# Feed-forward stages with one 512-column matmul for both activation parts, and a mixer whose silu gates stand before the attention

## The reference, cut to what matters

```python
def swiglu(h, w_gate, w_up, w_down):                 # four times, and once more in layer 0 of the second block
    return (jax.nn.silu(h @ w_gate) * (h @ w_up)) @ w_down      # 1024 -> 2816 -> 1024

# even mixer (once): three attention branches, softmax(q @ k.T * scale + mask) @ v, and a gated unit
# mixer of the second block (twice), from proj = h @ w_in[layer]:
y_a = (silu(rg) * rms_norm(retention(rq, rk, rv))) @ ret_w_out
y_b = (silu(hg) * rms_norm(hgrn2_scan(...)) * norm_g) @ hgrn_w_out
y_c = swa_with_sinks(sq, sk, sv, sinks) @ swa_w_out              # softmax attention, 16 heads
merged = sigmoid(ga) * y_a + sigmoid(gb) * y_b + sigmoid(gc) * y_c
mix = merged @ w_o
```

## Time and profile before

| what | value |
|---|---|
| median of three runs | 3395.35 us |
| the profiled execution | 3393.7 us |
| its span | 3391.8 us |
| mean granted TensorE clock | 0.961 |
| VectorE busy | 2269.6 us |
| ScalarE busy | 1820.6 us |

### The profile page before, as it was taken

The page is one execution under the profiler, slowest core; times in us unless marked ns, Lnnn a source line. Parts: engine busy times, 40 slices in busy tenths (PEclk is TensorE's granted clock), DMA queues, the critical chain, the costliest instruction groups (busy, mean ns, idle before and its releaser), DMA issues. The chain is left out here.

```text
span 3391.8 us, 49440 instructions
## 1 busy us (share of the span) xinstructions
PE 3141.8 (93%) x20206; PEld 2824.7 (83%) x20206; DVE 2269.6 (67%) x2478; ACT 1820.6 (54%) x2143; POOL 175.6 (5%) x101
## 2 busy tenths in 40 slices
PE   6998799998999899989899999897999999999996
PEld 6987699887689799879898998896888888888885
DVE  3455445787744556565545556645899899999997
ACT  3444444433244455464344455552777777777775
POOL 0000000002400001010000020100000000000000
PEclk9998899999999899989999999997999999999998
DMA  4552155443145433334454433333999999999995
GB/s 154 185 190 108 72 178 201 174 173 124 63 174 185 180 131 132 131 109 152 171 186 161 141 134 126 126 137 149 339 355 361 353 353 358 351 356 349 355 364 196
DMA packets 97410, 698.58 MB, mean 206 GB/s; under 512 B 10960, under 2 KB 11472, under 8 KB 13776
## 3 DMA queue, kind: packets, MB, share of 16 engines
q1 hardware_dynamic: 97232, 696.11, 56.5%
HBM read 693.97 MB, written 1.05 MB: 205 GB/s over the span
## 5 line engine op out<-in xcount | busy, mean ns | idle before, releaser
L854 PE MATMUL ps<-act_high,weight_low 128*128 128x256 f32 x3072 | 878.3, 286 | 0.0
L854 PE MATMUL ps<-act_high,weight_high 128*128 128x256 f32 x2624 | 757.0, 288 | 24.3 <-DVE weight_low L710 16.7
L854 PE MATMUL ps<-act_low,weight_high 128*128 128x256 f32 x2624 | 749.4, 286 | 0.0
L854 PEld LDWEIGHTS ps<-act_high,weight_low 128*128 128x128 f32 x3072 | 599.0, 195 | 0.0
L854 PEld LDWEIGHTS ps<-act_high,weight_high 128*128 128x128 f32 x2624 | 511.1, 195 | 34.9 <-issue 18.5
L854 PE MATMUL ps<-weight_low,act_high 128*128 128x512 f32 (+2 forms) x1456 | 515.3, 354 | 0.0
L854 PEld LDWEIGHTS ps<-act_low,weight_high 128*128 128x128 f32 x2624 | 511.1, 195 | 2.3 <-issue 0.2
L854 PE MATMUL ps<-weight_high,act_high 128*128 128x512 f32 (+2 forms) x1360 | 496.3, 365 | 13.7 <-DVE act_low L2655 3.9
L854 PE MATMUL ps<-weight_high,act_low 128*128 128x512 f32 (+2 forms) x1360 | 487.6, 359 | 0.0
L710 DVE TENSOR_TENSOR weight_low<-ring,weight_high 128x2048 fp32r<-128x2048 f32 x108 | 247.4, 2291 | 245.6 <-ACT weight_high L663 245.5
L663 ACT ACTIVATE weight_high<-ring 128x2048 fp32r<-128x2048 f32 x108 | 206.6, 1914 | 351.5 <-PE ps L854 351.5
(11 more groups left out here) (447 smaller groups left out, 5764.3 us busy)
## 6 DMA issues: line engine op xcount, KB each, us to landing
ring<-in_l_moe_up SPq DMA_DIRECT2D x110, 1024.0 KB, 6.0
ring_more<-in_l_moe_down SPq DMA_DIRECT2D x110, 1024.0 KB, 6.0
ring<-in_l_w_in SPq DMA_DIRECT2D x92, 1024.0 KB, 4.8
vtm<-in_l_moe_gate SPq DMA_DIRECT2D x55, 1024.0 KB, 6.0
merged<-in_l_moe_gate SPq DMA_DIRECT2D x55, 1024.0 KB, 6.1
ring<-in_l_ffn_down SPq DMA_DIRECT2D x52, 1024.0 KB, 4.8
ring<-in_l_ffn_up SPq DMA_DIRECT2D x35, 1024.0 KB, 4.8
ring_more<-in_l_ffn_gate SPq DMA_DIRECT2D x32, 1024.0 KB, 4.8
```

The costliest lines, as they stand in the source:

```text
L854: ins = nc.tensor.matmul(out, still[a], moving[b], start=first and n == 0, stop=last and n == 2, skip_group_check=True)
```

## The change

1. **Feed-forward, gate and up.** `act_high` and `act_low` become one tensor `c.act` (k, part, 256). One matmul `both_parts` moves 512 columns, high and low side by side, under the high weight into a whole bank; `high_part` moves 256 under the low weight into its first half. So 16 matmuls per half instead of 24. The bank's two halves are then summed by VectorE's `tensor_reduce` over pairs: `gate_sums` for the gate and the same in `products` for the up. ScalarE's silu and VectorE's product read the sums, and TensorE's banks come free with the sums.
2. **Feed-forward, order.** `clear` is gone: the first `down` starts its banks itself (the loop's first two bodies are peeled for that). At the start of a stage the third unit's high and low are made before the silus and the products, not behind them.
3. **Attention.** The next pass's scores wait for `read`, signalled by the mask addition, not for `biased`.
4. **Mixer.** HGATE moves from 38 to 32, SQ, SK, SV to 36, 40, 41, ATTEND from 38 to 42; the four `hg_split` stand at u = 34, 35, 39, 40. The silu gates get buffers of their own. GpSimd's loop is four gates, then eight weighings.
5. **Sigmoid gates** become tanh(x/2): `unload` takes tanh with scale 0.5, VectorE adds 1 in the same instruction that multiplies, and the factor of a half is applied where the merged sum is split.

```diff
@@ split_ffn_stage
-                nc.scalar.activation(silu[h], ps[:, 2 * h, 0:T], ACT.Silu).then_inc(silu_made.sem, 1)
+                nc.scalar.activation(silu[h], gate[h], ACT.Silu).then_inc(silu_made.sem, 1)
...
+            def gate_sums(n):
+                for h in range(2):
+                    dve.wait_ge(made.sem, n * 6 + (mb + h + 1))
+                    dve.wait_ge(silu_made.sem, n * 2 + (sb + h - 1))
+                    nc.vector.tensor_reduce(gate[h], halves(2 * h), axis=AX.X, op=ALU.add)\
+                        .then_inc(gate_made.sem, 1)
             def products(n):
                 for h in range(2):
+                    dve.wait_ge(made.sem, n * 6 + (mb + h + 3))
+                    nc.vector.tensor_reduce(rise[h], halves(2 * h + 1), axis=AX.X, op=ALU.add)\
+                        .then_inc(rise_made.sem, 1)
+                for h in range(2):
                     dve.wait_ge(silu_made.sem, n * 2 + (sb + h + 1))
-                    nc.vector.tensor_tensor(hidden[h], silu[h], ps[:, 2 * h + 1, 0:T], ALU.mult).then_inc(hidden_made.sem, 1)
+                    nc.vector.tensor_tensor(hidden[h], silu[h], rise[h], ALU.mult).then_inc(hidden_made.sem, 1)
...
             def start():
                 make_low(first[1])
+                gate_sums(0)
+                make_low(second)
                 products(0)
-                make_low(second)
             def triple(t):
                 hidden_lows(t.n, t.odd)
                 make_low(t.unit(1))
+                gate_sums(t.n + 1)
                 make_low(t.unit(2))
                 products(t.n + 1)
                 make_low(t.unit(3))
...
+                        both_parts(c, 2 * h + bank, still[0][0], 0)
+                        for k in range(KD):
+                            high_part(c, 2 * h + bank, still[k][1], k)
+                        for k in range(1, KD):
+                            last = both_parts(c, 2 * h + bank, still[k][0], k)
...
+def both_parts(c, bank, still, k):
+    return c.nc.tensor.matmul(c.ps[:, bank, :], still, c.act[:, k, :, :].rearrange("p s t -> p (s t)"), start=k == 0,
+                              stop=k == KD - 1, skip_group_check=True)
+def high_part(c, bank, still, k):
+    return c.nc.tensor.matmul(c.ps[:, bank, 0:T], still, c.act_high[:, k, :], start=False, stop=False, skip_group_check=True)
@@ even_stage and mixer_stage
-                    pe.wait_ge(biased.sem, biased.base + n)
+                    pe.wait_ge(read.sem, read.base + n)
@@ mixer_stage
-RQ, RK, RV, HF, HQ, HI, RG, GA, SQ, SK, SV, HGATE, GB, GC, SO, WO, UNITS = (
-    0, 2, 4, 8, 12, 16, 20, 24, 32, 36, 37, 38, 42, 50, 54, 58, 62)
-ROPE, RETAIN, PREPARE, RECUR, ROOT, ATTEND = 4, 7, (12, 24), (17, 29), (24, 36), 38
+RQ, RK, RV, HF, HQ, HI, RG, GA, HGATE, SQ, SK, SV, GB, GC, SO, WO, UNITS = (
+    0, 2, 4, 8, 12, 16, 20, 24, 32, 36, 40, 41, 42, 50, 54, 58, 62)
+ROPE, RETAIN, PREPARE, RECUR, ROOT, ATTEND = 4, 7, (12, 24), (17, 29), (24, 36), 42
+HG_SPLIT = (34, 35, 39, 40)
...
-                    take(gate[i % 2], ACT.Sigmoid)
+                    half_tanh(gate[i % 2])
```

More of the change, by code:

```diff
@@ L597, in split_ffn_stage @@
     ahead = Ahead(c, then, used) if then is not None else None
-    acts = (c.act_high, c.act_low)
     silu = [c.work[:, T * h:T * h + T] for h in range(2)]
     hidden = [c.work[:, T * (2 + h):T * (3 + h)] for h in range(2)]
+    gate = [c.work[:, T * (4 + h):T * (5 + h)] for h in range(2)]
+    rise = [c.work[:, T * (6 + h):T * (7 + h)] for h in range(2)]
+    halves = lambda bank: ps[:, bank, :].rearrange("p (s t) -> p t s", s=2)
     class Step:
@@ L606, in __init__ @@
             self.n, self.pair, self.odd = pair * 2 + odd, pair, odd
+            self.first = isinstance(pair, int) and pair == 0 and odd == 0
         def unit(self, j):
@@ L618, in stream @@
         else:
-            with eng.Fori(0, G // 2) as i:
+            body(Step(0, 0))
+            body(Step(0, 1))
+            with eng.Fori(1, G // 2) as i:
                 for odd in range(2):
@@ L768, in _ @@
         def _(pe):
[L769 to L773, removed]
             def split(u):
@@ L786, in across, with down @@
                     pe.wait_ge(freed.sem, n * 2 + (count + h - 1))
[L787 to L788 removed]
+                    still = [[m[:, k, P * h:P * h + P] for m in w] for k in range(KD)]
+                    if fresh and h == 0:
+                        for k in range(KD):
                             pe.wait_ge(norm.low.sem, norm.low.base + k + 1)
[L790 to L791 removed]
+                            if k < KD - 1:
+                                both_parts(c, 2 * h + bank, still[k][0], k)
+                            last = high_part(c, 2 * h + bank, still[k][1], k)
+                        last = both_parts(c, 2 * h + bank, still[KD - 1][0], KD - 1)
+                    else:
+                        both_parts(c, 2 * h + bank, still[0][0], 0)
+                        for k in range(KD):
+                            high_part(c, 2 * h + bank, still[k][1], k)
+                        for k in range(1, KD):
+                            last = both_parts(c, 2 * h + bank, still[k][0], k)
                     last.then_inc(made.sem, 3 if h == 1 and last_first else 1)
[L794 removed]
+            def down(u, n, odd, final=False, fresh=False):
                 w = [m.rearrange("p (h n) -> p h n", h=2) for m in split(u)]
@@ L816, in triple @@
                 across(t.unit(1), t.n + 1, 1)
-                down(t.unit(2), t.n, t.odd)
+                down(t.unit(2), t.n, t.odd, fresh=t.first)
             stream(pe, start, triple, lambda: down(after.unit(0), G - 1, 0, True))
@@ L1378, in even_stage @@
         s.advance(2)
-    for s in (scored, biased, exped, factored, weighted, probs, probs_taken, attended):
+    for s in (scored, read, biased, exped, factored, weighted, probs, probs_taken, attended):
         s.advance(PASSED)
```

110 lines of the change are left out of this document (57 added, 53 removed).

## The result

The kernel after takes 3354.62 us (median of four runs, 3353.27 to 3356.12), the kernel before in the same session 3396.9. The ratio is 0.9878, 95% interval 0.9863 to 0.9894. The forecast was 3360 in 3346 to 3391, faster.

A forecast was written before the change was run, and what follows sets the result against it. TensorE, busy 93% of the span, was taken as the bound, VectorE in parts of the third feed-forward stage, ScalarE and VectorE in mixer attention. 3393.7 - 23.5 (feed-forward) - 11 (mixers) = 3359, median said 3360, range 3346 to 3391.

The forecast's parts named there:

- Start: Start of each feed-forward stage: 2.8 us of waiting goes, a new stall of 0.7 comes, net 2.1 per stage.
- Sums: VectorE in feed-forward: 0.69 us per sum, free in four plain stages, third stage 3.5 us longer.
- (a): First body of the third feed-forward stage: a 5.1 us table piece and gate sums delay a low, stall 3.2 us.
- (b): Second body of the third feed-forward stage, with a table piece of 4.1 us: stall 1.1 us.
- Step (c): Third feed-forward stage, two bodies bound by VectorE take its work in full: 2 x 2.7 = 5.3 less TensorE's 0.4.
- (d): Third feed-forward stage, the two bodies behind the VectorE-bound ones, pieces of 2.5 to 3.3 us: about 1 us.
- Mixers: Two mixers' attention: seven steps 74.9 us instead of 78.2, first step about 2.2 shorter; 5.5 per mixer, 11 together.
- bound of 20: Upper bound of the mixers' gain, if TensorE's waits, 7.5 us in one mixer, go too.
- A: Rival: feed-forward sums cost VectorE 1.22 us each, feed-forward gives 3.0, kernel 3381 us; chance 0.10.
- B: Rival: 512-column matmuls cost 0.240 us, fixed price not saved, 22.9 us comes back, kernel 3383; chance 0.06.
- D: Rival: a sum costs 1.75 us, third feed-forward stage grows some 43, kernel 3418; decides from about 1.45; chance 0.05.
- C: Rival: the mixers give nothing, through odd steps' unloads and exps or a late recurrence; kernel 3371 us; chance 0.09.

The follow-up runs named there:

- e6: The kernel after with each 512-column matmul of gate and up made as two of 256 columns: 3376.13 us, ratio 0.994 to before.
- e4: The kernel before with only the start order of the five feed-forward stages changed and the zero matmuls gone: 3379.19 us, ratio 0.9955.
- the second profile: The kernel after once more, unchanged, on the chip of the kernels with even pieces: 3354.58 us, ratio 0.9884 to before.
- e5: The kernel after with each sum over pairs made twice, 1.37 us instead of 0.69: 3373.32 us, ratio 0.9932 to before.
- e9: The kernel after, third feed-forward stage with three 256-column matmuls per k-step, no sums, table instructions in 19 near-even pieces: 3345.11 us.
- e7: The kernel after with the two mixers' gates as ScalarE's Sigmoid again instead of tanh: 3355.05 us, ratio 0.9879 to before.
- e8: The kernel after with the attention's scores waiting for the scaled maximum (`biased`) again: 3355.21 us, ratio 0.988 to before.
- e2: The kernel before with only the attention and mixer part of the change, feed-forward as before: 3383.72 us, ratio 0.9971.
- e11: The kernel before once more, unchanged, for a second profile: 3396.11 us, one run.
- e10: The kernel after, 512-column matmuls and sums kept, third feed-forward stage's table instructions cut into 19 near-even pieces: 3346.56 us, ratio 0.9861 to before.
- e3: The kernel after, third feed-forward stage alone with three 256-column matmuls per k-step and no sums: 3352.61 us, ratio 0.9879 to before.

## Why the prediction was right, point by point

The direction and most terms held. The forecast median was 35 us under that of before; measured are 42 in the same session and 39 to 42 against all runs of before. Feed-forward and mixers gave 33.8 us in the traces where 34.5 were said, but several terms of that sum were off by 1 to 4 us and cancelled, which is luck.

**1. Matmuls.** Forecast 0.227 and a body of 16.55; measured 0.230 between `both_parts` and 16.61 for the bodies of the plain stages, so 0.37 us per body and not 0.43. At 11 groups that is 4.1 per stage and 20.4 in all instead of 22.9. The fixed price is there (e6: bodies of 16.98 again), but it is worth 0.012 us per matmul saved and not 0.013. The 2.5 ns that the Trainium skill ("TensorE: Matmul & The Clock Gate", "Back-to-back issue gap") gives for a matmul by itself would have given a body of 16.9; the trace decides against it.

**2. Start.** No zeros, and the new wait of 0.7 at the second up unit has a start distance of 0.84 us in all five stages, 0.6 above the normal one: as forecast. Net 2.1 was right: 4.1 + 2.1 = 6.2 stands against 6.3 in FF 2, 6.5 in FF 5 and 6.6 in the second profile's FF 1 (201.76; the first profile's 7.5 has 0.9 us more in the same code). In FF 4 the wait of before also cost clock (e4), and windows there would have shown it beforehand; with its 1.7 the stage's 8.0 comes out.

**3. Sums.** 0.685 us each, free in the plain stages (e5), as forecast. In FF 3 the waits (a) and (b) were forecast at 3.2 and 1.1; the start distances are 3.08 and 1.14, so 2.9 and 0.9 as waits. Step (c) was mis-sized: "its work in full: 2 x 2.7" was to add 4.9 us in two bodies. (By its own premise the 0.4 us that TensorE saves in each such body turn into waiting and had to be added, not taken off: 6.2.) TensorE's distances there were 2.67, 1.28 and 1.95 and are 4.33 and 3.33, 1.8 more; above the normal distance that is 2.0. VectorE was not full there: it was idle for 1.35 and 1.13 us of the windows in the earlier trace rows, and e9 shows that with the work cut evenly TensorE does not wait at all. (d) gave nothing (2.07 and 2.10). So waits add 5.8 us and not 10.2. In their place came what the prediction had not: behind the long waits TensorE runs at its lower clock, 4.0 us above before by the 22 and 3 doubled distances. -4.1 - 2.1 + 5.8 + 4.0 = +3.6, measured +4.6; 1 us stays open. That the forecast was +3.5 is luck: two errors that cancel, waits put 4.4 us too high and a clock that was put at nothing. The clock of FF 3 was never taken out by itself; that the waits cause its fall is argued from where it falls, and e6's wait of 3.60 us without a fall shows that it need not.

**4. Mixers.** Seven steps of 74.9 us were forecast, 74.91 is measured, and the single steps are those of the sum: five of 9.33 and 12.1, the first two 10.91 and 9.06, 1.5 us less for the copies that they lack. The step before them is 1.95 shorter, 2.2 was said. 5.2 per mixer by the steps, 5.2 by the length of mixer 1. The bound of 20, that TensorE's waits for the statistics go, was none: they went, but TensorE waited for the turned probabilities beside them already, and does so longer in after. The waits of before there, among them, are 15.9 us together, those of after 13.8. First the two lines of before that the earlier trace rows lacks, then after:

```profile
PE ps L2226 <- ACT rowbuf L2429: 7.2, 3, 2.5
PE ps L2226 <- ACT work L2429: 1.2, 1, 1.2
```

```profile
PE ps L2265 <- ACT rowbuf L2469: 9.1, 3, 3.9
PE ps L2265 <- ACT work L2469: 3.2, 2, 3.0
PE ps L2255 <- DVE work L2677: 1.5, 1, 1.5
```

Tanh gives nothing (e7), the wait for `read` neither (e8), so the order of the units is what is left of the part that e2 tests; no run changes the order alone.

**5. Read wait.** Zero (e8: +0.6, inside the scatter of the runs, 3352.82 to 3357.35).

**What the sum lacked.** 33.8 of the 40.4 us by which the two profiled spans differ are feed-forward and mixers (-23.7 and -10.1 with 4.85 in mixer 2, whose length in before's own two traces is 494.1 and 492.6). 2.3 in the odd stage are its clock, which differs between two executions of the same kernel by more than that (e11). The even mixer's 1.2 and the 3.0 of the experts lie in code that is the same or has no effect, and both are within what these stages differ by from trace to trace: the even mixer has 167.7 to 169.9 us in its new form and 168.8 to 170.3 in its old one, and the experts, whose code is the same in all fourteen traces, 1052 to 1059. Here all of these fell to the change's side; why they differ is open.

The rivals: A, B and D are excluded by the rows (0.685 us per sum, 0.230 per matmul), C by e2. D's threshold was too low (e5), and its 13.3 us of VectorE work in a body of the third stage stand in no row; the earlier trace rows have 15.6 and 15.9.

## What to carry to other kernels

Work added to an engine with room is free only where it is not bunched: compare the sum of an engine's work with the body, and then the longest piece with the slack at its place. Here cutting the pieces more evenly gave 7.5 us with three matmuls in FF 3 (3352.61 to 3345.11) and 8.0 with sums (3354.58 to 3346.56); which form is better there these runs do not tell. When a change adds waits to TensorE, read the granted clock behind them as well: long waits can cost a second time, which ten short ones did not.

## What the runs showed of the hardware

- A matmul of 512 activation columns that follows one with another stationary starts 0.230 us after it, one with 512 weight columns 0.227; 256 columns 0.120.
- `tensor_reduce` over pairs out of the matmul banks, 512 elements in and 256 out, takes 0.685 us, the time of a reduction of 512 elements to 4 (0.69 in the earlier trace rows) and not of a product with 256 out (0.42 in the earlier trace rows).
- TensorE's clock fell behind a wait of 3.9 us in FF 3 of after (0.57 and 0.75 in two windows of 5 us) and behind the next long one (start distance 3.33, 0.70), but not behind one of 3.6 us in the same place in e6 (1.00), nor behind the ten of up to 1.4 us in e10. Behind a wait of 2.4 us in the same place it fell in e4 (0.79, 0.87) and not in before and e3; behind the 2.3 us at the zeros in FF 4 and, by the windows of before, in no other stage. The Trainium skill, "TensorE: Matmul & The Clock Gate", part "The HAM clock gate", says of the rise behind a run's first matmuls that its point differs from run to run. The odd stage's 16.0 and 22.6 us for the same kernel are a difference of that kind, behind pauses in mid-kernel.
- A table load of 1.28 us is all that ScalarE shows for a switch: at the first stage's start the load at 41.15 is followed by the silu at 42.44.
